# Three Strassen pairs for the attention projection of a decoder layer, with two of the four weight sums of each pair on GpSimd

## Chip, cores and metric

The kernel runs on one core of a Trainium2 chip. The metric is the device time of one execution in microseconds (us), the median of repeated runs. Times inside an execution are us from the start of its span.

## What is computed

One decoder layer over 256 tokens of width 1024, in float32. The part that matters here is the first half: a projection of the normalised tokens, two token mixers fed by it, and the joining of their outputs.

```python
xn = rms_norm(h, norm_mix[i])
proj = jnp.einsum('bsd,de->bse', xn, w_in[i])
gdn_qkv, gdn_z, gdn_a, gdn_b, fox_qkv, fox_f, merge = split_cols(proj, IN_SPLITS)
qkv = jax.nn.silu(causal_depthwise_conv(gdn_qkv, conv_w[i]))
...
o_a = gated_delta_rule(q_a, k_a, v_a, log_alpha, beta)
...
q_f = rms_norm(fox_qkv[..., :FOX_W].reshape(B, S, FOX_HEADS, FOX_HD), q_norm[i])
...
o_f = forgetting_attention(q_f, k_f, v_f, log_f)
...
h = h + jnp.einsum('bsd,de->bse', gate_a * y_a + gate_f * y_f, w_out[i])
h = h + routed_moe(...)
```

`fox_qkv` is the projection of the attention: 3072 columns, six weight tiles of 512 columns. `gated_delta_rule` needs, for each of 16 problems (8 heads, two chunks of 128 tokens), the inverse of a unit lower triangular matrix. The mixture of experts and a gated embedding follow, and fill the rest of the time.

## The kernel before

Each engine has its program written out by hand, in order; semaphores join them. Nothing is scheduled automatically: the order of the code in each engine's block is the order of execution, and a wait at the head of an engine's queue holds everything behind it.

**Weights.** Twenty-two tiles of 1024 rows by 512 columns (2 MB each) of the projections pass through a ring of three slots (`wring`, `A_SLOTS = 3`), filled by SyncE in `load(t)` (L466). A slot is filled again when its last reader on TensorE is done. Tiles 0 to 5 are the delta rule's q, k, v; tiles 6 to 11 the attention's; 12 and 13 the gate z; then the merge gates and the three output projections.

**Plain tiles.** In `project` (L1018) a weight tile is used twice, once for each 128 tokens: 8 chunks of the contraction, each one a 128x128 by 128x512 product. One such float32 product shows in the trace as two MATMUL records, so one `project` is 16 records. Before the change the attention's six tiles run this way: twelve `project` calls, fox.0.0 to fox.5.1, whose results ScalarE copies out of the accumulating bank.

**Paired tiles.** z, the merge gates and the output projections take two tiles at a time in a Strassen-Winograd form (`product`, L1028): seven half products of 4 chunks (8 records) instead of eight. They are named by number: 1, 5, 2, 6, 3, 7, 4 is their usual order. On VectorE `token_sums` makes four sums of token blocks once for each left factor, `weight_sum(p, k)` (L1848 to L1859) makes four sums of weight halves (128x2048 each) for every pair, and `join(p, k)` (L1869 to L1882) puts products together. ScalarE keeps products 1 and 5 in memory (`keep`). Product 5 waits for weight sum 1, product 6 for sum 2, product 7 for sum 3 and for join 6, product 4 for sum 4. Half products open banks A, C, B, D of a pair; a bank has to be drained before it is opened again.

**Beside the attention's tiles.** Between its products TensorE does small work for the delta rule (`BESIDE_FOX`: transposes tq, key products kk, spread rows bb, query products qk), which VectorE scales. Then, on VectorE, a **solve** of 31 steps inverts the sixty-four diagonal 32x32 blocks (L1825 and L1827, two small instructions a step, each waiting for the one before). SyncE brings the blocks through memory first (`box_blocks`, L490 and L492) and the inverses back (`unbox_inverses`, L497 and L502) into `xi` and `vi`, which GpSimd has set to zero (L667, L668). TensorE then completes the inverses by blocks (P5, X5, V5, P6, V6: L1187 and L1194), between z's seven products.

Of the kernel before, what the change touches and what calls it, by code (L numbers as in the profile page):

```python
# [41 lines left out]
def bc(ap, axis, n):  # L42
# [12 lines left out]
BESIDE_FOX = {(0, 0): ["tq.0.5", "tq.1.5", "kk.0", "kk.1"], (0, 1): ["bbT", "kk.2", "kk.3"],  # L55
              (1, 0): ["bb.0", "bb.1", "bb.2", "bb.3"], (1, 1): ["qk.0", "qk.1"], (2, 0): ["qk.2", "qk.3"]}

PAIRED = ("z", "m0", "m2", "ya", "yf", "wo")
Z_, M0_, M2_, YA_, YF_, WO_ = range(6)
LEFT = (0, 0, 0, 1, 2, 3)  # L60
# [11 lines left out]
def bank_fills():  # L72
# [8 lines left out]
    for j in range(6):  # L81
        for n in range(NT):
            f += [f"fox.{j}.{n}"] + BESIDE_FOX.get((j, n), [])
    f += ["cT", "P5", "z.A", "X5", "V5", "z.C", "P6.0", "P6.1", "V6.0", "V6.1", "z.B", "z.D"]
# [9 lines left out]
    g = [(name, ALL_BANKS) for name in f]  # L94
# [34 lines left out]
def program(nc, x, p, norm_mix, w_in, conv_w, a_log, dt_bias, gdn_norm, fox_f_bias, q_norm, k_norm,  # L129
# [3 lines left out]
    with ctx:  # L133
# [221 lines left out]
        ya_gated = sem("ya_gated")  # L355
        u_made, c11_made, activated = sem("u_made"), sem("c11_made"), sem("activated")
# [17 lines left out]
        wtiles += [(w_in2, C_FOX + WT * j, f"fox.{j}.1") for j in range(6)]  # L374
# [5 lines left out]
        W_QKV, W_FOX, W_PAIRED = 0, 6, 12  # L380

        def halves_of(p):

            k = W_PAIRED + 2 * p
            b0, b1 = wring[k % A_SLOTS], wring[(k + 1) % A_SLOTS]
            return b0[:, LO, :], b1[:, LO, :], b0[:, HI, :], b1[:, HI, :]

# [58 lines left out]
        def _(sp):  # L446
# [3 lines left out]
            def load(t):  # L450
# [43 lines left out]
            def unbox_inverses():  # L494
# [3 lines left out]
                sp.wait_ge(zeroed, 2)  # L498
# [70 lines left out]
            sp.wait_ge(t_made, 4 * WO_ + 4)  # L569
# [53 lines left out]
        def _(pool):  # L623
# [43 lines left out]
            g.memset(xi[:, :, :], 0.0).then_inc(zeroed, 1)  # L667
            g.memset(vi[:, :, :], 0.0).then_inc(zeroed, 1)  # L668
# [3 lines left out]

# [1701 lines left out]
```

## Time and profile before

| | |
|---|---|
| median of three runs | 905.59 us (905.34 to 906.22) |
| the profiled execution | 906.76 us, its span 905.0 us |
| TensorE busy | 893.1 us, 99% of the span |
| VectorE busy | 498.6 us, 55% |
| ScalarE busy | 198.1 us, 22% |
| GpSimd busy | 48.1 us, 5% |
| TensorE clock granted | 0.999 of full speed |

TensorE is never idle for long; its busy share says where the time is, but not whether another engine is nearly late. The stage of this change lies from about 104 to 229 us: the attention's projection up to 196 us, then z and the blocks of the inverses.

### The profile page before, as it was taken

How to read it: one execution, taken by the hardware profiler on the slowest of the kernel's cores; microseconds unless marked ns; L12 is line 12 of the kernel's file. 1: busy time of each engine (PE TensorE's matmuls, PEld its weight loads, DVE VectorE, ACT ScalarE, POOL GpSimd, SP SyncE). 2: the span in 40 equal slices, each digit the busy share in tenths (PEclk: the TensorE clock that was granted, in tenths of full speed). 3: DMA queues.
4: the chain of work that ended last, by engine and by line, in shares of the span. 5: the costliest groups of instructions: out<-in, count | busy, mean ns of one | idle time of the engine just before them, and what ended most of it. 6: DMA issues, size and time to landing. Idle time of an engine off the chain costs nothing.

```text
span 905.0 us, 21061 instructions
## 1 busy us (share of the span) xinstructions
PE 893.1 (99%) x9194; PEld 510.3 (56%) x9194; DVE 498.6 (55%) x954; ACT 198.1 (22%) x401; POOL 48.1 (5%) x72
## 2 busy tenths in 40 slices
PE   8999999999999999999999999999999999999997
PEld 6888755455845554446555555545455555555543
DVE  3656735964586887866434354443434444445367
ACT  2214200022417561233111111111111111111122
POOL 4011100050020000020000000000000000000010
PEclk9999999999999999999999999999999999999999
DMA  8643424562241528988999999999999999999951
GB/s 251 209 166 102 178 94 145 180 208 95 94 138 50 185 94 321 365 347 297 405 419 423 420 422 423 421 423 423 420 422 423 423 422 422 421 421 423 416 202 48
DMA packets 65587, 266.10 MB, mean 294 GB/s; under 512 B 11353, under 2 KB 14026, under 8 KB 41098
## 3 DMA queue, kind: packets, MB, share of 16 engines
q1 hardware_dynamic: 65530, 265.54, 74.4%
q8 instruction: 27, 0.44, 0.2%
q14 instruction: 14, 0.11, 0.0%
q10 hardware_dynamic: 16, 0.00, 0.0%
HBM read 263.69 MB, written 1.84 MB: 293 GB/s over the span
## 4 chain that ended last, share of the span: by engine, by line
PE 95%; DVE 2%; ACT 1%; issue 1%; DMA 0%; POOL 0%; DVEq 0%; ACTq 0%; POOLq 0%
PE bank L1493 25%; PE bank L1028 15%; PE bank L1474 13%; PE bank L1137 9%; PE bank L1018 9%; PE bank L1444 5%; PE bank L1457 5%; PE bank L1602 2%; PE bank L1005 2%; PE bank L1091 2%; PE bank L1513 1%; PE bank L1402 1%; PE bank L1413 1%; PE bank L1232 1%; PE bank L1330 1%; ACT arena L722 1%
## 5 line engine op out<-in xcount | busy, mean ns | idle before, releaser
L1493 PE MATMUL bank<-arena 128*32 128x256 f32 x4096 | 227.2, 379 | 0.3 <-DVE arena L2180 0.3
L1493 PEld LDWEIGHTS bank<-arena 128*32 128x32 f32 x4096 | 132.8, 110 | 100.5 <-issue 18.6
L1474 PE MATMUL bank<-arena 128*32 128x512 f32 x1024 | 116.5, 595 | 0.5 <-ACT arena L935 0.5
L1028 PE MATMUL bank<-arena 128*128 128x512 f32 x248 | 111.1, 598 | 0.0
L1137 PE MATMUL bank<-actT,arena 128*128 128x256 f32 x384 | 85.3, 380 | 0.0
L1018 PE MATMUL bank<-arena,actT 128*128 128x512 f32 x192 | 83.5, 593 | 0.0
L1137 PEld LDWEIGHTS bank<-actT,arena 128*128 128x128 f32 x384 | 72.0, 190 | 10.2 <-issue 0.8
L1028 PEld LDWEIGHTS bank<-arena 128*128 128x128 f32 x248 | 45.8, 190 | 53.9 <-issue 53.8
L933 ACT ACTIVATE arena<-bank 128x256 f32<-128x256 f32 x32 | 12.3, 384 | 267.9 <-PE bank L1493 267.9
L722 ACT ACTIVATE arena<-bank 128x512 f32<-128x512 f32 (+2 forms) x69 | 35.5, 534 | 154.5 <-PE bank L1018 82.7
L2231 DVE COPY arena<-bank 128x512 f32<-128x512 f32 x32 | 22.1, 692 | 81.9 <-PE bank L1474 81.9
L2216 DVE SCALAR_TENSOR_TENSOR arena<-arena,gslot,bank 128x256 f32<-128x256 f32 x32 | 15.4, 480 | 90.0 <-ACT arena L933 90.0
L1474 PEld LDWEIGHTS bank<-arena 128*32 128x32 f32 x1024 | 30.0, 109 | 59.9 <-issue 57.5
L1018 PEld LDWEIGHTS bank<-arena,actT 128*128 128x128 f32 x192 | 36.0, 190 | 43.2 <-issue 43.0
L2221 DVE COPY arena<-bank 128x512 f32<-128x512 f32 x31 | 21.4, 692 | 67.9 <-PE bank L1444 67.9
L1444 PE MATMUL bank<-onehot,arena 128*128 128x64 bf16 x1536 | 50.0, 193 | 0.0
L1444 PEld LDWEIGHTS bank<-onehot,arena 128*128 128x128 bf16 x1536 | 49.0, 98 | 1.0 <-issue 0.7
L2247 DVE TENSOR_TENSOR arena<-arena,masks 128x1024 f32<-128x1024 f32 x31 | 38.0, 1226 | 1.1
L653 POOL TENSOR_SCALAR stat<-stat 128x1 f32<-128x1 f32 x6 | 1.6, 268 | 617.7 <-ACT arena L971 468.3
L1005 PE MATMUL bank<-ident,arena 128*128 128x128 f32 (+1 forms) x206 | 29.4, 286 | 4.7 <-DMA arena<-in_norm_mix 3.3
L939 ACT ACTIVATE arena<-bank 128x512 f32<-128x512 f32 x32 | 19.1, 597 | 66.1 <-PE bank L1474 66.1
L1005 PEld LDWEIGHTS bank<-ident,arena 128*128 128x128 f32 (+1 forms) x206 | 25.1, 147 | 14.5 <-issue 10.6
(321 smaller groups left out, 1006.4 us busy)
## 6 DMA issues: line engine op xcount, KB each, us to landing
arena<-in_we_gate SPq DMA_DIRECT2D x32, 2048.0 KB, 17.3
arena<-in_we_up SPq DMA_DIRECT2D x31, 2048.0 KB, 18.5
arena<-in_we_down SPq DMA_DIRECT2D x29, 2048.0 KB, 17.5
arena<-in_w_in SPq DMA_DIRECT2D x17, 2048.0 KB, 8.1
arena<-in_we_down SPq DMA_DIRECT2D x6, 1024.0 KB, 8.9
arena<-in_w_branch_gdn SPq DMA_DIRECT2D x2, 2048.0 KB, 7.8
arena<-in_w_branch_fox SPq DMA_DIRECT2D x2, 2048.0 KB, 8.9
arena<-in_w_out SPq DMA_DIRECT2D x2, 2048.0 KB, 10.0
```

The costliest lines, as they stand in the source:

```text
L722: a.activation(dst, ps(name)[:, 0:cols_used] if len(dst.shape) == 2 else ps(name)[:, 0:cols_used].rearrange("p (a b) -> p a b", a=dst.shap ...
L1005: ins = t.transpose(o[0:w, i * P:i * P + rows_in], v, ident[0:rows_in, 0:rows_in])
L1018: ins = t.matmul(o[:, :], lhs[:, c, n * P:n * P + P], w[:, c, :], start=(c == 0), stop=(c == KC - 1))
L1028: ins = t.matmul(o[:, :], lhs[:, c, :], rhs[:, c, :], start=fresh and c == 0, stop=c == HC - 1, skip_group_check=not fresh)
L1137: ins = t.matmul(o[:, i * S:i * S + S], w[:, c, col:col + P], actT[:, c, :], start=(c == 0), stop=(c == KC - 1))
L1444: ins = t.matmul(bank[5 + half][:, c * P + n * 2 * CAP:c * P + (n + 1) * 2 * CAP], hparts[:, k, n, (4 * half + c) * P:(4 * half + c + 1) * P],
L1457: ins = t.matmul(bank[2 * n + j][:, :], spread[s][hp, :], yparts[j][k][hp, :], start=False, stop=False, skip_group_check=True)
L1474: ins = t.matmul(bank[4 + j][i * CAP:i * CAP + CAP, :], hidT[:, c, i * CAP:i * CAP + CAP], d_in[s][:, i % 2, c * D + WT * j:c * D + WT * j ...
L1493: ins = t.matmul(bank[4][i * CAP:i * CAP + CAP, m * DE:m * DE + DE], xg[:, c, i * CAP:i * CAP + CAP], gu_in[s][:, m, i % 2, c * DE:c * DE ...
L2221: v.tensor_copy(xg[:, 4:8, :], bank[6][:, :].rearrange("p (c s) -> p c s", c=4)).then_inc(xb_ready, 1)
L2231: v.tensor_copy(y[:, WT:D], bank[5][:, :]).then_inc(y_ready[1], 1)
L2247: v.tensor_tensor(y, y, yhigh, ALU.subtract).then_inc(y_rest, 1)
```

## The change

The attention's six tiles become three pairs f0, f2 and f4 with `product`, so that `project` is no longer used for them. The signs of the Strassen form are turned so that weight sums are all additions. For the three new pairs GpSimd makes weight sums 1 and 3 (`add_first`, `add_third`), VectorE makes sums 2 and 4. Banks are dealt out apart during the stage: 0, 1, 2 for the pairs and 3 to 7 for the work beside. On VectorE the solve is moved ahead of the scaling of the queries and keys (L1810 to L1817), and has joins and sums of the pairs between its steps. The zeroing of `xi` and `vi` is moved from the start to behind the pairs' last products, since the weight differences of f0 and f4 use the memory of `xi` and kept products of f2 that of `vi`. On TensorE product 1 of z now stands ahead of P5.

```diff
+FOX_BANKS, SIDE_BANKS = (0, 1, 2), (3, 4, 5, 6, 7)
+FOX_ORDER = ((0, 1, ["tq.0.5", "tq.1.5", "kk.0", "kk.1"]), (0, 2, []), (0, 5, ["bbT", "kk.2", "kk.3"]), (0, 6, []), (0, 3, ["bb.0", "bb.1", "bb.2", "bb.3"]),
+             (0, 7, ["qk.0", "qk.1"]), (0, 4, []), (1, 1, ["qk.2", "qk.3"]), (1, 5, []), (1, 2, []), (1, 6, []), (1, 3, []), (1, 7, []), (1, 4, []),
+             (2, 1, []), (2, 5, []), (2, 2, []), (2, 6, []), (2, 3, []), (2, 7, []), (2, 4, []))
...
+        wdif = [at(lo, HC * WT).rearrange("p (c n) -> p c n", c=HC) for lo in (TX, RZ, TX, R1, R1, TV, TPB, R1 + 2048)]
...
-            g.memset(xi[:, :, :], 0.0).then_inc(zeroed, 1)
-            g.memset(vi[:, :, :], 0.0).then_inc(zeroed, 1)
...
+            def add_first(p):
+                b00, b01, _, _ = halves_of(p)
+                for tile in (W_PAIRED + 2 * p, W_PAIRED + 2 * p + 1):
+                    pool.wait_ge(w_loaded[tile % A_SLOTS], 16 * (tile // A_SLOTS + 1))
+                g.tensor_tensor(wdif[p], b00, b01, ALU.add).then_inc(sum1_made, 1)
+
+            def add_third(p):
+                _, b01, _, b11 = halves_of(p)
+                pool.wait_ge(sum1_made, p + 1)
+                g.tensor_tensor(b01, b11, b01, ALU.add).then_inc(sum3_made, 1)
+
             for i, (j, n) in enumerate(TQ_ORDER):
+                if i == 6:
+                    add_first(F0_)
+                if i == 7:
+                    add_third(F0_)
...
+            add_first(F2_)
+            add_third(F2_)
+            wait_filled(pool, "f0.D")
+            add_first(F4_)
+            add_third(F4_)
+            pool.wait_ge(c11_made, F2_ + 1)
+            g.memset(vi[:, :, :], 0.0).then_inc(zeroed, 1)
+            wait_filled(pool, "f4.D")
+            g.memset(xi[:, :, :], 0.0).then_inc(zeroed, 1)
...
-            for j in range(6):
-                w = weights(W_FOX + j)
-                for n in range(NT):
-                    project(f"fox.{j}.{n}", w, n)
-                    for name in BESIDE_FOX.get((j, n), []):
-                        beside(name)
+            for p, k, names in FOX_ORDER:
+                product(p, k)
+                for name in names:
+                    beside(name)
...
+            product(Z_, 1)
             pe.wait_ge(xv_loaded, 16 * 2 * NB)
             corner32("P5", lambda b, q: (lT[q:q + BLK, b, q + BLK:q + 2 * BLK], q + BLK), lambda b, q: xi[q:q + BLK, b, q:q + BLK])
-            product(Z_, 1)
...
+            JOINED, SUMMED = {8: 6, 13: 3, 17: 7, 21: 4}, {24: 2, 27: 4}
+            for k in range(BLK - 1):
+                m = BLK - 1 - k
+                outer = rank1[:, 0:m * (k + 1)].rearrange("p (i j) -> p i j", i=m)
+                seq(v.tensor_tensor(outer, bc(lb[:, k, k + 1:BLK], 2, k + 1), bc(xb[:, k, 0:k + 1], 1, m), ALU.mult))
+                below = xb[:, k + 1:BLK, 0:k + 1]
+                seq(v.tensor_tensor(below, below, outer, ALU.subtract))
+                if k in JOINED:
+                    join(F2_, JOINED[k])
+                if k in SUMMED:
+                    weight_sum(F4_, SUMMED[k])
```

TensorE at the end of the attention's tiles, before (L1018 the last plain tile, L1011 the transpose cT, L1187 P5 and X5, L1028 z's product 1):

```order
L1018 MATMUL bank6<-arena,actT 128x512 [waits drained6]
L1018 MATMUL bank6<-arena,actT 128x512 x7
L1011 MATMUL bank7<-identb,cf3 48x128 [waits drained7,cf_split]
L1011 MATMUL bank7<-identb,cf3 48x128
L1187 MATMUL bank0<-arena 32x32 [waits drained0,xv_loaded]
L1187 MATMUL bank0<-arena 32x32 x31
L1028 MATMUL bank1<-arena,actT 128x512 [waits drained1,w_loaded0]
L1028 MATMUL bank1<-arena,actT 128x512 x3
L1187 MATMUL bank2<-arena 32x32 [waits drained2,drained0]
L1187 MATMUL bank2<-arena 32x32 x31
```

and the same place in the change (L1066 products, the first of them f4's product 4, L1049 cT, L1229 P5 and X5):

```order
L1066 MATMUL bank2<-arena,actT 128x512 [waits drained2,t_made]
L1066 MATMUL bank2<-arena,actT 128x512 x3
L1049 MATMUL bank4<-identb,cf3 48x128 [waits drained4,cf_split]
L1049 MATMUL bank4<-identb,cf3 48x128
L1066 MATMUL bank5<-arena,actT 128x512 [waits drained5,w_loaded0]
L1066 MATMUL bank5<-arena,actT 128x512 x3
L1229 MATMUL bank6<-arena 32x32 [waits drained6,xv_loaded]
L1229 MATMUL bank6<-arena 32x32 x31
L1229 MATMUL bank7<-arena 32x32 [waits drained7,drained6]
L1229 MATMUL bank7<-arena 32x32 x31
```

z's product 1 stood between P5 and X5; now it stands ahead of P5, and X5 (which waits for bank 6, P5's) follows P5 at once.

VectorE around the eighteenth step of the solve, before:

```order
L1825 TENSOR_TENSOR arena<-arena 64x252 [waits dve_step]
L1827 TENSOR_TENSOR arena<-arena 64x14x18 [waits dve_step]
L1825 TENSOR_TENSOR arena<-arena 64x247 [waits dve_step]
L1827 TENSOR_TENSOR arena<-arena 64x13x19 [waits dve_step]
L1825 TENSOR_TENSOR arena<-arena 64x240 [waits dve_step]
```

and in the change (L1928 and L1930 the steps, L1881 and L1884 join 7 of f2):

```order
L1928 TENSOR_TENSOR arena<-arena 64x252 [waits dve_step]
L1930 TENSOR_TENSOR arena<-arena 64x14x18 [waits dve_step]
L1881 TENSOR_TENSOR arena<-arena,bank0 128x512 [waits filled0,dve_step]
L1884 TENSOR_TENSOR arena<-arena 128x512 [waits drained0,kept]
L1928 TENSOR_TENSOR arena<-arena 64x247
L1930 TENSOR_TENSOR arena<-arena 64x13x19 [waits dve_step]
L1928 TENSOR_TENSOR arena<-arena 64x240 [waits dve_step]
```

Join 7 of f2, which drains bank 0 (f2.B, and next f4.C), now stands behind eighteen steps of the solve.

TensorE where the attention's tiles begin, before and (second fence) in the change; L1005 and L1043 are the transposes tq.1.4:

```order
L1005 MATMUL bank3<-ident,arena 128x128 [waits drained3,conv_done]
L1005 MATMUL bank3<-ident,arena 128x128 x3
L1018 MATMUL bank4<-arena,actT 128x512 [waits drained4,w_loaded0]
L1018 MATMUL bank4<-arena,actT 128x512 x7
L1005 MATMUL bank5<-ident,arena 128x128 [waits drained5,conv_done]
```

```order
L1043 MATMUL bank3<-ident,arena 128x128 [waits drained3,conv_done]
L1043 MATMUL bank3<-ident,arena 128x128 x3
L1066 MATMUL bank0<-arena,actT 128x512 [waits drained0,w_loaded0]
L1066 MATMUL bank0<-arena,actT 128x512 x3
L1043 MATMUL bank3<-ident,arena 128x128 [waits drained3,conv_done]
```

The first product of the stage opened bank 4; now it opens bank 0, whose last user is qkv.11, the last convolution tile.

## Rows read from the trace of the kernel before

**Rows 1.** The page's busy times of the engines.

```profile
PE 893.1 (99%) x9194; PEld 510.3 (56%) x9194; DVE 498.6 (55%) x954; ACT 198.1 (22%) x401; POOL 48.1 (5%) x72
```

**Rows 2.** The chain that ended last, in order of time: start, length, what.

```profile
104.21 6.87 PE bank L1018 x16
...
137.69 1.78 PE bank L1091 x16
...
148.13 48.07 PE bank L1018 x112
196.42 1.13 PE bank L1187 x64
197.55 3.63 PE bank L1028 x8
...
214.89 13.93 PE bank L1028 x32
```

**Rows 3.** VectorE's timeline ahead of the stage, and a weight load of SyncE.

```profile
98.86 2.48 DVE L1767 TENSOR_TENSOR arena<-arena,masks 128x512 f32<-128x512 f32 x4
...
103.74 2.54 DVE L1704 SCALAR_TENSOR_TENSOR arena<-bank,cols,arena 128x255 f32<-128x255 f32 x6
...
L466 SPq DMA_DIRECT2D arena<-in_w_in x1: 367/367/367, 88.2 to 88.2; - x1
```

**Rows 4.** VectorE's timeline: the solve, its copy, a weight sum, a join.

```profile
152.04 0.17 DVE L1825 TENSOR_TENSOR arena<-arena 64x31 f32<-64x31 f32 x1
...
165.28 0.41 DVE L1827 TENSOR_TENSOR arena<-arena 64x252 f32<-64x252 f32 x1
...
171.09 0.33 DVE L1827 TENSOR_TENSOR arena<-arena 64x175 f32<-64x175 f32 x1
...
174.67 0.18 DVE L1827 TENSOR_TENSOR arena<-arena 64x31 f32<-64x31 f32 x1
174.89 1.05 DVE L1828 COPY arena<-arena 64x1024 f32<-64x1024 f32 x1
...
192.22 2.29 DVE L1848 TENSOR_TENSOR arena<-arena 128x2048 f32<-128x2048 f32 x1 [3.82 <-DMA arena<-in_w_in]
...
218.63 0.69 DVE L1869 TENSOR_TENSOR arena<-arena,bank 128x512 f32<-128x512 f32 x1 [3.44 <-PE bank L1028]
```

**Rows 5.** GpSimd's timeline, and the VectorE instruction beside its last row.

```profile
11.25 1.80 POOL L667 MEMSET arena<- 128x2048 f32 x1
...
190.62 5.44 POOL L685 TENSOR_TENSOR f_ri<-f_ri,nhalf 128x32 f32<-128x32 f32 x1
247.31 0.22 POOL L689 TENSOR_TENSOR stat<-stat 128x16 f32<-128x16 f32 x1 [51.26 <-DVE stat L1939]
247.61 2.29 POOL L690 TENSOR_TENSOR stat<-stat 128x16 f32<-128x16 f32 x1
...
247.53 2.29 DVE L1855 TENSOR_TENSOR arena<-arena 128x2048 f32<-128x2048 f32 x1 [0.30 <-PE bank L1028]
```

**Rows 6.** SyncE's timeline, landings of transfers, and a page row of loads.

```profile
138.27 5.22 SPq L490 DMA_DIRECT2D lbox<-arena  x4
147.06 0.54 SPq L492 DMA_DIRECT2D arena<-lbox  x1
...
180.12 1.93 SPq L502 DMA_DIRECT2D arena<-xbox  x4
182.09 2.08 SPq L502 DMA_DIRECT2D arena<-vbox  x4
...
DMA to landing us min/median/max: 2.0/2.3/2.5
...
arena<-in_w_in SPq DMA_DIRECT2D x17, 2048.0 KB, 8.1
```

**Rows 7.** ScalarE's timeline: the two copies that drain P5.

```profile
197.60 1.19 ACT L774 ACTIVATE arena<-bank 32x512 f32<-32x512 f32 x2 [0.77 <-PE bank L1187]
```

More of the change, by code:

```diff
@@ L373, in program @@
         wtiles = [(w_in2, C_QKV + WT * t, f"qkv.{2 * t + 1}") for t in range(6)]
-        wtiles += [(w_in2, C_FOX + WT * j, f"fox.{j}.1") for j in range(6)]
+        wtiles += [(w_in2, C_FOX + WT * j, f"f{j // 2 * 2}") for j in range(6)]
         wtiles += [(w_in2, C_Z + WT * j, "z") for j in range(2)]
@@ new lines, in weight_sum @@
+            def weight_sum(p, k):
+                b00, b01, b10, b11 = halves_of(p)
+                if k == 1:
+                    for i in range(2):
+                        tile = W_PAIRED + 2 * p + i
+                        dve.wait_ge(w_loaded[tile % A_SLOTS], 16 * (tile // A_SLOTS + 1))
+                    ins = v.tensor_tensor(wdif[p], b01, b00, ALU.add)
+                if k == 3:
+                    dve.wait_ge(t_made, sums_made(p, 1))
+                    ins = v.tensor_tensor(b01, b11, b01, ALU.add)
+                if k == 2:
+                    if p < Z_:
+                        tile = W_PAIRED + 2 * p + 1
+                        dve.wait_ge(w_loaded[tile % A_SLOTS], 16 * (tile // A_SLOTS + 1))
+                        dve.wait_ge(sum1_made, p + 1)
+                    else:
+                        dve.wait_ge(t_made, sums_made(p, 1))
+                    dve.wait_ge(half_filled, 3 * p + 1)
+                    ins = v.tensor_tensor(b00, b11, wdif[p], ALU.add)
+                if k == 4:
+                    dve.wait_ge(t_made, sums_made(p, 2))
+                    dve.wait_ge(half_filled, 3 * p + 2)
+                    ins = v.tensor_tensor(wdif[p], b10, b00, ALU.add)
+                ins.then_inc(t_made, 1)
@@ L1884, in _, with fox_squares @@
-            token_sums(LEFT[Z_])
+            join(F4_, 3)
+            join(F4_, 7)
+            join(F4_, 4)
+            for p in (F0_, F2_):
+                for q in "ACBD":
+                    wait_drained(dve, f"{PAIRED[p]}.{q}")
+            dve.wait_ge(c11_made, F2_ + 1)
+            def fox_squares(n, half):
+                src = fox[:, n, D * half:D * half + D]
+                seq(v.tensor_tensor(at(TPB, 1024), src, src, ALU.mult))
+                ins = v.tensor_reduce(f_ss[:, n, 16 * half:16 * half + 16], at(TPB, 1024).rearrange("p (a b) -> p a b", a=16), AX.X, ALU.add)
+                if half:
+                    ins.then_inc(fss, 1)
+                    dve.wait_ge(fss, n + 1)
+                else:
+                    seq(ins)
@@ L1885, in _ @@
+            weight_sum(Z_, 1)
+            weight_sum(Z_, 3)
             for n in range(NT):
                 for half in range(2):
-                    for j in range(2):
-                        wait_drained(dve, f"fox.{2 * half + j}.{n}")
-                    src = fox[:, n, D * half:D * half + D]
-                    seq(v.tensor_tensor(at(TPB, 1024), src, src, ALU.mult))
-                    ins = v.tensor_reduce(f_ss[:, n, 16 * half:16 * half + 16], at(TPB, 1024).rearrange("p (a b) -> p a b", a=16), AX.X, ALU.add)
@@ L1893, in _ @@
[L1893 to L1899 removed]
+                    fox_squares(n, half)
             wait_filled(dve, "cT")
@@ L2090, in _ @@
             dve.wait_ge(kept, 2 * WO_ + 1)
-            k = [step(onto(n, j, m1[WO_])) for n, j in BLOCKS[1:]]
+            k = [step(onto(n, j, m1[WO_], ALU.subtract if j else ALU.add)) for n, j in BLOCKS[1:]]
             wait_filled(dve, "wo.A")
```

194 lines of the change are left out of this document (95 added, 99 removed).

## The prediction

> **What bounds the kernel now.** I read the page's busy times first: TensorE works for 99% of the span [rows 1]. So only two things count, how much work TensorE loses, and how long it newly waits. The chain of work in order of time gives both scales for this stage [rows 2]. A plain tile half (16 records) takes 6.87 us; the stage begins at 104.21 and its last seven come in one piece of 48.07 us, 6.87 each. The half products of z take 3.48 us each when they follow one another (13.93 for four) and 3.63 between small work. Then I read the timelines of the others, for what could be late.
>
> **The work removed.** Twelve plain halves, 12 x 6.87 = 82.4 us, become 21 half products, 21 x 3.48 = 73.1. TensorE gains 9.3 us. Nothing else in the stage leaves TensorE; the work beside (91.99 from 104.21 to 196.20, less 82.4: 9.6, of which the last piece takes 1.8) is the same.
>
> **The work added elsewhere.** VectorE gets four token sums (only moved), six weight sums of 2.29 us and fifteen instructions of 0.69 for joins [rows 4], about 24 us more. ScalarE makes six copies more and eight fewer. What follows asks where TensorE waits. Times are on the clock of the trace of before.
>
> 1. *Entry.* f0.A opens bank 0, which qkv.11 used last. VectorE drains that with six instructions that end at 103.74 + 2.54 = 106.28 [rows 3]; TensorE arrives at 104.0. Before, bank 4 was long free. Wait: **2.3 us**.
>
> 2. *Exit, zeroing.* `xi` can only be zeroed once product 4 of f4 is complete, and SyncE's eight transfers into `xi` and `vi` wait for it. 0.2 release, 1.80 for the memset [rows 5], 0.1, then issues: eight, from 180.12 to 184.17, the last landing about 2.3 after its issue, 5.9 in all [rows 6]. Sum 8.0. TensorE has cT (0.22) and z's product 1 (3.63) as cover, 3.85. Wait: **4.2 us**. Before, both memsets were done at 15 us and the inverses were back 10 us ahead of P5 (186 against 196.42).
>
> 3. *Exit, P5.* X5 waits for ScalarE's two copies of P5, 1.19 us [rows 7], plus 0.26 for two releases. z's product 1 covered them and now stands ahead. Wait: **1.45 us**.
>
> 4. *Solve and joins.* The solve starts behind f2's product 5 and sum 4. With the entry's wait, TensorE starts f2's product 5 at 106.3 + 24.4 (seven products) + 7.7 (work beside) + 3.5 (f2's product 1) + 1.8 (the last piece beside) = 143.8; it ends at 147.3, the sum at 149.7. SyncE's boxes are no obstacle: started at about 133, they are in at the latest 13.8 us later (138.27 to 152.04). The eighteen steps before join 7 take 165.69 - 152.04 = 13.65 [rows 4], the joins at steps 8 and 13 0.7 each, join 7 itself 0.7: bank 0 is free at about 165.5. TensorE wants it for f4's product 5 at 143.8 + 7 x 3.48 = 168.1. Margin 2.6 us (2.3 with releases): no wait, but nothing to spare. At the end f4's join 6 stands behind the last steps, sum 4 and the copy, about 7.5 us after sum 2, where TensorE has two products, 6.96. Wait: **0.5 us**.
>
> 5. *Two GpSimd adds per pair.* No such instruction is in the trace. Lower bound of one: the memset of the same shape, 1.80, which moves one operand where an add moves three [rows 5]; upper bound three passes, 5.4. Reads alone through one door would make two, 3.6. I take 4.5, midway between two and three passes. By time alone they fit: f4's second tile is requested after f2's product 6 (154.2), lands 8.1 later [rows 6], sum 1 is ready at 166.8, wanted at 168.1.
>
> What matters is whether they leave VectorE alone. At 247.61 a GpSimd multiply of 128x16, whose neighbour took 0.22, took 2.29: it ended with VectorE's two-input sum that had started at 247.53 [rows 5]. So the two share something that one holds to its end. Whether GpSimd holds it against VectorE too is the open point. For it: the sharing is complete in the case seen. Against: VectorE's sum at 192.22 took its normal 2.29 while a GpSimd power ran from 190.62 to 196.06 [rows 4, 5]. But that one reads 32 elements and then computes; an add of 2048 reads nearly all the time. I take it that the long add does hold. The Trainium skill, "SBUF — State Buffer", section "Who interferes with whom", speaks against this change: a VectorE instruction with two SBUF inputs and a GpSimd one that reads SBUF exclude each other for the whole instruction, whoever starts first. The trace agrees in one direction (2.29 for 0.22), and shows no long GpSimd read for the other. For the length, "GPSIMD Engine Reference", section 3.1, gives 4.497 us for this very add (by it the sum would be the same), and no run here shows it yet.
>
> The price of holding:
> - f0's first add starts when its tile lands, about 96, and holds until 100.5. VectorE's four two-input instructions at 98.86 [rows 3] start 1.6 late; 0.9 of it is idle time before the last convolution. Entry wait **+0.7**.
> - f2's adds fall among scaling instructions with one SBUF input; they shift one join's last part and sum 2, and cost the solve's start 0.4 at most.
> - f4's adds (162.3 to 171.4) fall into the solve, where nearly every instruction has two SBUF inputs. VectorE stands still for 2 x 4.5 = 9.0. Join 7 is 9.0 later, less the margin of 2.3: f4's product 5 waits **6.7**. From join 7 to the end of sum 2 VectorE needs 0.7 + 5.7 (steps 18 to 24, to 171.42) + 0.7 + 2.29 = 9.4, against two products, 6.96: product 6 waits **2.5**.
>
> **Sum.** Without holding: -9.3 + 2.3 + 4.2 + 1.45 + 0.5 = -0.9. With it: -0.9 + 0.7 + 6.7 + 2.5 = +9.0. The profiled execution of before took 906.76, 1.2 over the median of 905.59; its like after would be 915.8, and the median **914.6 us**.
>
> **Rivals.**
> - *GpSimd's add holds nothing* (chance 0.25). For it: the power of 190.62. Against: the complete wait at 247.61. The kernel is then not slower: 905.6 - 0.9 = **904.7**, and TensorE's waits are those of 1 to 4. It decides from a hold of about 1.2 us per add on; below that the margin of 2.3 swallows it.
> - *More is late than that* (0.12): an add of 5.4 (+0.9 on each of two, and f2's product 7 then waits 0.7 too) and tiles landing 1 us later since the boxes' transfers run beside them: +12.5, **918.1**. For it: the loads now come in twos. Against: 8.1 was measured with pauses between and beside boxes too.
> - *The gain shows after all* (0.06): if waits 2 and 3 were covered, by transfers landing as a group rather than one by one, 905.6 - 0.9 - 3 = **901.7**. Against: the eight issues themselves take 4.05 us.
> - That the seven-for-eight exchange does not happen has no chance worth a number: the counts of products are in the program.
>
> **Numbers.** The forecast has 0.57. Its own range is 911 to 917 (adds of 3.6 to 5.0). The whole range reaches to the case without holding and leaves out the edges: 904 to 918.5. A change of this kernel can be told from none at about 0.2%, 1.8 us. Slower by more: 0.57 + 0.12 = 0.69; within: nearly all of the 0.25, 0.23; faster: 0.06 and a tail of the second, 0.08.
>
> **What the profile after would show.** Right: TensorE idle 3 us at its first half product of the stage, released by VectorE's convolution; GpSimd adds of 4.5 us (start to start); during the two of f4 VectorE's small solve instructions stretched to 4.5 us each, twice; TensorE waiting about 7 us at f4's product 5 for VectorE's join 7; 4 us ahead of P5 for a transfer; 1.5 ahead of X5 for ScalarE. If the solve's instructions keep their 0.4 us beside GpSimd's adds, the first rival holds. If P5 starts within 4 us of cT, step 2 is wrong. If the first product waits for nothing, step 1 is. If the half products take 3.63 rather than 3.48, the gain is 3 us smaller.

## The result, and the profile after

| | before | after |
|---|---|---|
| median of four runs | 905.47 us (905.22 to 906.22) | 919.31 us (919.05 to 919.68) |
| ratio | 1 | 1.0152, 95% interval 1.0140 to 1.0164 |
| profiled execution, its span | 906.76, 905.0 us | 919.38, 917.7 us |
| TensorE clock granted, mean | 0.999 | 0.987 |
| TensorE busy | 893.1 us, 99% | 891.7 us, 97% |

The change makes the kernel 1.5% slower. The forecast was 914.6 us, and its range ended at 918.5: the sign was right, the size too small by 4.7 us. Of the runs further below, one of the four executions of e10_tuned took 1856.62 us and is in none of its figures.

The page of the changed kernel, its busy times and the clock in 40 slices of 22.9 us. [Rows 1] have the first line before.

```profile
PE 891.7 (97%) x9170; PEld 510.3 (56%) x9170; DVE 534.3 (58%) x975; ACT 196.3 (21%) x398; POOL 76.2 (8%) x78
...
PEclk9999999897999999999999999999999999999999
```

TensorE has 1.4 us less to do by its busy time although seven half products stand for eight, since some of its work ran longer: in two slices, from 161 to 184 and from 206 to 229 us, the clock digit is not 9.

TensorE's waits in the whole program, summed by line and releaser. The rows left out are before the stage (2.3 and 1.6 us) and after it, and one of 0.9 ahead of the last record of V5 (214.30), which the account below has in the length of X5 and V5.

```profile
PE bank L1066 <- DVE arena L1881: 5.8, 1, 5.8
PE bank L1229 <- DMA arena<-vbox: 4.1, 1, 4.1
PE bank L1066 <- DVE arena L1746: 2.8, 1, 2.8
...
PE bank L1229 <- ACT arena L801: 1.3, 1, 1.3
```

They are the waits of the prediction, in its places: join 7 of f2, the transfers into `vi`, the last convolution (L1746), ScalarE's copies of P5. Its TensorE timeline in the stage (L1043 transposes, L1066 half products, L1229 P5, X5 and V5); [rows 2] have the same places before:

```profile
103.55 1.47 PE L1043 MATMUL bank<-ident,arena 128*128 128x128 f32 x12
107.77 3.67 PE L1066 MATMUL bank<-arena,actT 128*128 128x512 f32 x8 [2.75 <-DVE arena L1746]
...
174.92 6.72 PE L1066 MATMUL bank<-arena 128*128 128x512 f32 x8 [5.83 <-DVE arena L1881]
181.47 3.60 PE L1066 MATMUL bank<-arena,actT 128*128 128x512 f32 x8
184.91 10.46 PE L1066 MATMUL bank<-arena 128*128 128x512 f32 x24
...
206.76 1.92 PE L1229 MATMUL bank<-arena 32*32 32x32 f32 x64 [4.10 <-DMA arena<-vbox]
209.96 3.44 PE L1229 MATMUL bank<-arena 32*32 32x32 f32 x127 [1.29 <-ACT arena L801]
...
214.43 5.75 PE L1066 MATMUL bank<-arena 128*128 128x512 f32 x8
220.12 2.08 PE L1236 MATMUL bank<-arena 64*64 64x64 f32 x32
...
241.59 0.60 PE L1043 MATMUL bank<-ident,arena 128*128 128x128 f32 x4
```

Read the starts, not the lengths: f4's product 5 starts at 174.92 and the next at 181.47, 6.55 us, where three others take 10.30 together (184.91 to 195.21). z's product 5 takes 5.69 (214.43 to 220.12). X5 and V5 take 4.47 (209.96 to 214.43). The clock of those stretches (columns: stretch, length, busy time and records of PE, PEld, DVE, ACT, POOL, the clock, DMA share, GB/s):

```profile
174.90:181.50 6.60, 6.58 (x9) 2.75 (x10) 6.15 (x16) 0.00 (x0) 1.81 (x1) 0.53 0.01 2
181.50:203.00 21.50, 21.16 (x51) 8.95 (x49) 18.07 (x27) 1.50 (x3) 1.81 (x1) 1.00 0.39 129
203.00:206.70 3.70, 0.00 (x0) 0.00 (x0) 3.63 (x4) 0.29 (x1) 0.00 (x0) 0.76 0.84 122
206.70:214.40 7.70, 5.46 (x192) 5.09 (x192) 7.50 (x8) 2.36 (x4) 5.27 (x2) 0.50 0.70 264
214.40:220.10 5.70, 5.70 (x9) 2.23 (x8) 2.10 (x1) 1.18 (x2) 5.53 (x3) 0.63 0.01 3
```

Before each of the two long waits ends the granted clock falls to 0.5, the level of 1.2 GHz (in windows of 1 us: at about 174.2 and 204.9). It is back at 1.00, 2.4 GHz, only at about 181, 6 us into product 5, and at about 218.6, 12 us behind the second wait. This the prediction had not priced. The VectorE and GpSimd timelines of the same execution show who made TensorE wait; [rows 4] have the solve before, [rows 3] the instruction at 98.86 before (2.48):

```profile
99.66 4.13 DVE L1809 TENSOR_TENSOR arena<-arena,masks 128x512 f32<-128x512 f32 x4
...
163.00 0.42 DVE L1928 TENSOR_TENSOR arena<-arena 64x256 f32<-64x256 f32 x1
163.45 4.62 DVE L1930 TENSOR_TENSOR arena<-arena 64x256 f32<-64x256 f32 x1
168.10 4.60 DVE L1928 TENSOR_TENSOR arena<-arena 64x255 f32<-64x255 f32 x1
...
174.09 0.69 DVE L1881 TENSOR_TENSOR arena<-arena,bank 128x512 f32<-128x512 f32 x1
```

```profile
163.27 4.52 POOL L684 TENSOR_TENSOR arena<-arena 128x2048 f32<-128x2048 f32 x1 [19.50 <-DMA arena<-in_w_in]
167.87 4.56 POOL L689 TENSOR_TENSOR arena<-arena 128x2048 f32<-128x2048 f32 x1
...
198.87 1.81 POOL L712 MEMSET arena<- 128x2048 f32 x1 [21.43 <-PE bank L1066]
```

A solve instruction that takes 0.42 us takes 4.62 and its successor 4.60: each ends 0.3 us behind the GpSimd add beside it (those end at 167.79 and 172.43). Join 7 follows at 174.09, and its first half ends where TensorE's wait does.

**The account.** For a measure that the rest of the program does not touch I take the stage, from the twelve transposes ahead of it to the transposes tg behind z. Before:

```profile
102.74 1.47 PE L1005 MATMUL bank<-ident,arena 128*128 128x128 f32 x12
...
201.11 1.83 PE L1187 MATMUL bank<-arena 32*32 32x32 f32 x109
...
203.55 3.70 PE L1028 MATMUL bank<-arena 128*128 128x512 f32 x8
...
228.66 0.60 PE L1005 MATMUL bank<-ident,arena 128*128 128x128 f32 x4
```

That is 228.66 - 102.74 = 125.92 us before and 241.59 - 103.55 = 138.04 after, +12.12. The stage itself began 0.81 later; TensorE's program ahead of it is the same in both.

| term, us | predicted | measured |
|---|---|---|
| entry wait | 2.3 + 0.7 | 2.75 |
| f4's product 5 waits | 6.7 | 5.83 |
| f4's product 5 at the slower clock | 0 | 6.55 - 3.44 = 3.11 |
| products 6 and 7 wait | 2.5 + 0.5 | 0 |
| wait ahead of P5 | 4.2 | 4.10 |
| wait ahead of X5 | 1.45 | 1.29 |
| P5 slower (1.91 for 1.13) | 0 | 0.78 |
| X5 and V5 slower (4.47 for 2.44) | 0 | 2.03 |
| z's product 5 slower (5.69 for 3.63) | 0 | 2.06 |
| sum of these | 18.35 | 21.95 |
| seven half products for eight | -9.3 | 12.12 - 21.95 = -9.8 |

A half product takes 3.44 us from start to start (10.30 / 3), so the exchange should give 82.4 - 21 x 3.44 = 10.2; 9.8 is what is left over. In each further profile below, the waits and slow products, less this 9.8, make the measured stage within 0.4 us.

### The profile page after: what moved, and what is told of

It reads as the page before. It is cut to its first block, busy times and chain, and to the rows that moved or that the text cites. A ratio compares the mean times of both kernels' runs of the same rounds, so it can differ in the third digit from the quotient of the medians.

```text
span 917.7 us, 21076 instructions
## 1 busy us (share of the span) xinstructions
PE 891.7 (97%) x9170; PEld 510.3 (56%) x9170; DVE 534.3 (58%) x975; ACT 196.3 (21%) x398; POOL 76.2 (8%) x78
## 4 chain that ended last, share of the span: by engine, by line
PE 90%; DVE 6%; ACT 1%; issue 1%; DMA 1%; POOL 0%; SPq 0%; DVEq 0%; ACTq 0%; POOLq 0%
PE bank L1535 24%; PE bank L1066 21%; PE bank L1516 12%; PE bank L1181 8%; PE bank L1486 5%; PE bank L1499 5%; PE bank L1644 2%; PE bank L1043 2%; PE bank L1135 2%; PE bank L1555 1%; DVE arena L1930 1%; DVE arena L1928 1%; PE bank L1444 1%; PE bank L1455 1%; PE bank L1274 1%
## 5 line engine op out<-in xcount | busy, mean ns | idle before, releaser
L1066 PE MATMUL bank<-arena 128*128 128x512 f32 x344 | 158.8, 613 | 5.8 <-DVE arena L1881 5.8
L1066 PEld LDWEIGHTS bank<-arena 128*128 128x128 f32 x344 | 65.6, 195 | 85.8 <-issue 85.5
L1066 PE MATMUL bank<-arena,actT 128*128 128x512 f32 x144 | 65.0, 596 | 2.8 <-DVE arena L1746 2.8
L753 ACT ACTIVATE arena<-bank 128x512 f32<-128x512 f32 (+2 forms) x60 | 30.1, 524 | 84.1 <-PE bank L1043 40.9
L1066 PEld LDWEIGHTS bank<-arena,actT 128*128 128x128 f32 x144 | 26.6, 190 | 33.8 <-issue 33.6
L1043 PE MATMUL bank<-ident,arena 128*128 128x128 f32 (+1 forms) x206 | 29.4, 286 | 4.3 <-DMA arena<-in_norm_mix 2.3
L807 ACT ACTIVATE arena<-bank 128x512 f32<-128x512 f32 x18 | 10.7, 595 | 106.2 <-PE bank L1066 106.2
L977 ACT ACTIVATE arena<-bank 128x512 f32<-128x512 f32 x32 | 19.1, 597 | 66.1 <-PE bank L1516 66.1
```

The lines of the kernel that those rows point to most:

```text
L753: a.activation(dst, ps(name)[:, 0:cols_used] if len(dst.shape) == 2 else ps(name)[:, 0:cols_used].rearrange("p (a b) -> p a b", a=dst.shap ...
L977: a.activation(y[:, 0:WT], bank[4][:, :], ACT.Copy).then_inc(y_ready[0], 1)
L1043: ins = t.transpose(o[0:w, i * P:i * P + rows_in], v, ident[0:rows_in, 0:rows_in])
L1066: ins = t.matmul(o[:, :], lhs[:, c, :], rhs[:, c, :], start=fresh and c == 0, stop=c == HC - 1, skip_group_check=not fresh)
```

## The experiments

All edits are to the changed kernel. "Stage" is the profiled length between the same two groups of transposes.

| run | median, us (lowest to highest) | ratio to before | stage, us |
|---|---|---|---|
| after | 919.31 (919.05 to 919.68) | 1.0152 | 138.04 |
| e1_short | 909.98 (908.88 to 910.96) | 1.0048 (1.0032 to 1.0065) | 129.88 |
| e2_long | 909.52 (909.16 to 909.93) | 1.0044 (1.0027 to 1.0061) | 130.39 |
| e11_copy | 911.44 (910.46 to 914.13) | 1.0059 (1.0037 to 1.0082) | 132.64 |
| e4_xi | 917.29 (916.06 to 920.0) | 1.0126 (1.0110 to 1.0143) | 139.43 |
| e5_fill | 916.74 (914.84 to 917.92) | 1.0129 (1.0112 to 1.0146) | 135.32 |
| e3_bank | 917.58 (916.06 to 918.34) | 1.0125 (1.0101 to 1.0148) | 136.67 |
| e6_vadds | 916.36 (914.04 to 917.1) | 1.0108 (1.0082 to 1.0134) | 136.87 |
| e8_order | 911.35 (909.12 to 911.96) | 1.0061 (1.0040 to 1.0082) | 129.86 |
| e9_all | 902.09 (901.71 to 903.55) | 0.9963 (0.9948 to 0.9977) | 122.37 |
| e10_tuned | 901.82 (900.32 to 902.49) | 0.9941 (0.9922 to 0.9961) | 122.88 |

The kernel before ran beside each group: 905.18, 905.23 and, beside e10 and e11, 906.38 us.

### Does GpSimd's add hold VectorE, and what in it does?

**e1_short**: the adds become one memset each.

```diff
-                g.tensor_tensor(wdif[p], b00, b01, ALU.add).then_inc(sum1_made, 1)
+                g.memset(wdif[p], 0.0).then_inc(sum1_made, 1)
...
-                g.tensor_tensor(b01, b11, b01, ALU.add).then_inc(sum3_made, 1)
+                g.memset(b01, 0.0).then_inc(sum3_made, 1)
```

> Each of the six GpSimd adds is replaced by one GpSimd memset of the same 128x2048 target, which reads nothing; all waits and signals stay. The kernel leaves out the three pairs' first and third weight sums. Theory A, that the long add holds VectorE: VectorE's solve instructions keep 0.42 us, join 7 of f2 is 9 us earlier, f4's product 5 waits for nothing and takes 3.44 to 3.5 us, the entry wait falls from 2.75 to 2.1, while the waits ahead of P5 (4.1) and X5 (1.3) and the slow stretch behind them stay. That takes off 5.8 + 3.1 + 0.7 = 9.6: 919.3 - 9.6 = 909.7 us, 908.5 to 911. Rival B, that f2's joins are late for another reason (the solve begins late, the loads are late, or TensorE is slow there of itself): 917 us or more, with the same 5 us wait.

**e2_long**: three memsets, longer than the add but without a read.

```diff
-                g.tensor_tensor(wdif[p], b00, b01, ALU.add).then_inc(sum1_made, 1)
+                for i in range(3):
+                    ins = g.memset(wdif[p], 0.0)
+                    if i < 2:
+                        seq(ins)
+                ins.then_inc(sum1_made, 1)
...
```

> Each of the six GpSimd adds is replaced by three memsets of its target one after the other (3 x 1.8 = 5.4 us, longer than the add's 4.5), still without any read. The kernel leaves out the three pairs' first and third weight sums. Theory A, that it is the two reading inputs of the GpSimd instruction that hold VectorE's: no VectorE instruction is stretched, f4's weight sums come 1.8 us later, which costs f4's product 5 at most 1 us: 909.7 to 911.5 us. Rival B, that any GpSimd instruction that occupies its engine so long holds VectorE, or that the length of the sums is what is waited for: 5.4 instead of 4.5 us held twice, 919.3 + 2 = 921 us or more.

**e11_copy**: one input instead of two.

```diff
-                g.tensor_tensor(wdif[p], b00, b01, ALU.add).then_inc(sum1_made, 1)
+                g.tensor_copy(wdif[p], b00).then_inc(sum1_made, 1)
...
-                g.tensor_tensor(b01, b11, b01, ALU.add).then_inc(sum3_made, 1)
+                g.tensor_copy(b01, b11).then_inc(sum3_made, 1)
```

> The changed kernel with each of the six GpSimd adds replaced by a GpSimd copy of the same size (one input instead of two). The kernel leaves out the three pairs' first and third weight sums, and copies one operand instead. It tells what in GpSimd's reading holds VectorE. Theory A, any GpSimd instruction that reads holds VectorE's two-input instructions to its end: solve instructions stretched to the copy's own length (1.8 to 3.6 us by the memset's 1.8 and the add's 4.5), f4's product 5 waits the less the shorter the copy is; at 3 us twice: 919.3 - 2 x 1.5 = 916 us, 914 to 917.5. Theory B, only two reading inputs hold: no instruction is stretched, as with memsets: 909 to 911 us.

Measured: 909.98, 909.52 and 911.44. With memsets both theory A held, 0.3 us from its value in e1 and 0.2 below its range in e2, and both rivals fell. GpSimd's timeline in e2, three memsets that begin at 162.56 (three more follow at 168.15), and a VectorE row beside them, one of twenty-odd alike:

```profile
162.56 5.53 POOL L685 MEMSET arena<- 128x2048 f32 x3 [16.09 <-DMA arena<-in_w_in]
```

```profile
162.36 0.42 DVE L1936 TENSOR_TENSOR arena<-arena 64x256 f32<-64x256 f32 x1
```

Eleven microseconds of GpSimd work stretch nothing; in e1 and e2 f4's product 5 has no wait. In e11 GpSimd's copy for f4's sum 1 (the one for sum 3 follows at 164.65 with 1.97), then VectorE's two instructions beside the two copies:

```profile
162.69 1.90 POOL L684 COPY arena<-arena 128x2048 f32<-128x2048 f32 x1 [23.51 <-DMA arena<-in_w_in]
```

```profile
162.77 2.08 DVE L1930 TENSOR_TENSOR arena<-arena 64x256 f32<-64x256 f32 x1
164.89 1.99 DVE L1928 TENSOR_TENSOR arena<-arena 64x255 f32<-64x255 f32 x1
```

One input is enough: VectorE's two-input instruction is held for the copy's whole 1.9 us. So theory A of e11 is right in its mechanism and B is wrong; its time was off because the copy is hardly longer than a memset (1.90 for 1.80 us), and 911.44 lies outside both ranges, 0.4 above B's: the time alone would not have told the two apart, the stretched instructions do. With 2.08 + 1.99 us instead of 4.62 + 4.60, f4's product 5 waits 0.7 for join 7, and product 6 shows the wait for sum 2, 2.2 us. The Trainium skill, "SBUF — State Buffer", section "Who interferes with whom", states just this condition, that a two-input VectorE instruction contends only with a GpSimd one that reads SBUF. These runs agree in all three cases: 0.42 us beside memsets, 2.08 beside a copy, 4.62 beside an add. One row does not fit the condition, and decides there: the GpSimd power reads SBUF too, and from 190.62 to 196.06 it held nothing, since VectorE's sum at 192.22 took its usual 2.29 [rows 4, 5]. Which GpSimd instructions hold to their end is shown here only for the add and the copy of 128x2048.

### Are the slow products the clock?

**e5_fill**: work that nothing reads stands in the two long waits.

```diff
             for p, k, names in FOX_ORDER:
+                if (p, k) == (F4_, 5):
+                    wait_drained(pe, "bb.3")
+                    for _ in range(56):
+                        t.transpose(bank[3][:, 0:P], ident[:, :], ident[:, :])
                 product(p, k)
...
             product(Z_, 1)
+            wait_drained(pe, "bb.3")
+            for _ in range(36):
+                t.transpose(bank[3][:, 0:P], ident[:, :], ident[:, :])
             pe.wait_ge(xv_loaded, 16 * 2 * NB)
```

> TensorE gets work that nothing uses in the two long waits: 56 transposes of 128x128 ahead of f4's product 5, 36 ahead of P5, into a bank that is free, with the waits themselves unchanged. Nothing is left out. Theory, that the slow products behind the waits (f4's product 5 at 6.55 instead of 3.44 us, X5 and V5 at 4.5 instead of 2.4, z's product 5 at 5.7 instead of 3.6) are the granted clock of an engine that has stood still: they come back to full speed in part or whole, and the granted clock stays at 0.9 or over there. Of the 8.0 us so lost, the 3.1 at f4's product 5 cover waits for sum 2 and join 6 of 2.5 + 0.5, so they give only 0.1 to 0.6; the other 4.9 are free. 919.3 - 5.3 = 914 us; 913 to 916. Rival, that the products are slow from something else (contention with transfers or with VectorE's work): no change, 919.3 us or more.

Measured 916.74 (the profiled execution 914.84), mean clock 0.996 for 0.987. Its TensorE timeline:

```profile
167.10 6.28 PE L1220 MATMUL bank<-ident 128*128 128x128 f32 x56
173.21 3.60 PE L1066 MATMUL bank<-arena 128*128 128x512 f32 x8
176.65 3.60 PE L1066 MATMUL bank<-arena,actT 128*128 128x512 f32 x8
182.38 12.23 PE L1066 MATMUL bank<-arena 128*128 128x512 f32 x24 [2.14 <-issue]
...
208.25 2.32 PE L1233 MATMUL bank<-arena 32*32 32x32 f32 x128 [1.29 <-ACT arena L801]
210.50 5.11 PE L1066 MATMUL bank<-arena 128*128 128x512 f32 x8
```

Where TensorE was kept at work until the wait ended, what follows is at full speed: product 5 takes 3.44 again, P5 1.20, X5 and V5 2.25. That the slow products are the clock, and the clock follows from the standing still, is shown; contention is out, since the work of VectorE, GpSimd and the transfers beside them is the same. Two more things are to be seen. Product 6 now waits 2.14 us for sum 2: this is the prediction's 2.5, which in the changed kernel was hidden behind the slow product 5. And the clock falls behind the shorter waits instead: 1.76 at product 6 (12.07 to the next start, for 10.31), 1.4 at z's product 5. So the filling gave back less than the 5.3 us expected: 2.6 by the medians, 0.7 above the theory's range, and 2.7 of the stage.

The Trainium skill, "TensorE: Matmul & The Clock Gate", section "HAM oscillation — how this bites in real kernels", describes that each burst behind a wait for data starts at the lower level. The windows above agree for the two long waits: 0.53 and 0.50 behind 5.8 and 4.1 us, where the page's two levels would be 0.5 and 1. They don't for every wait: the first half product behind 2.75 us ran at 1.00.

### The exit

**e4_xi**: `xi` is zeroed early.

```diff
-        wdif = [at(lo, HC * WT).rearrange("p (c n) -> p c n", c=HC) for lo in (TX, RZ, TX, R1, R1, TV, TPB, R1 + 2048)]
+        wdif = [at(lo, HC * WT).rearrange("p (c n) -> p c n", c=HC) for lo in (TX, RZ, R1, R1, R1, TV, TPB, R1 + 2048)]
...
             wait_filled(pool, "f0.D")
+            g.memset(xi[:, :, :], 0.0).then_inc(zeroed, 1)
+            wait_filled(pool, "qk.3")
             add_first(F4_)
...
-            wait_filled(pool, "f4.D")
-            g.memset(xi[:, :, :], 0.0).then_inc(zeroed, 1)
```

(Its sum tile went to R1, which z's own sum tile uses later, not to f2's RZ as the expectation has it, and f4's sum 1 waits for qk.3 as well. What the place itself does to the time was not tried; e9 has RZ.)

> The sum tile of f4 moves from xi's place to the one f2 used, so that xi can be zeroed by GpSimd once product 4 of f0 is done (ahead of f4's sums) instead of product 4 of f4; the adds stay. Theory: the wait ahead of P5 (4.1 us) is gone since the transfers of xi and vi land some 6 us earlier, and the half-speed clock behind it goes with it (0.8 in P5, 2.0 in X5 and V5, 2.1 in z's product 5). The 1.3 us wait for ScalarE stays, with some of the clock loss perhaps. 919.3 - 4.1 - 4.9 = 910.3 us; 909.5 to 912.5. Rival, that the fall of the clock at 203 comes late from the 5.8 us wait at 169 to 175 and not from the waits at 203 to 210: only the wait goes, 915.2 us.

Measured 917.29: two microseconds of nine, and neither the theory's range nor the rival's 915.2. The wait ahead of P5 fell only from 4.10 to 2.02, and what follows was as slow as before (X5 and V5 4.75 us, z's product 5 6.69). (The profiled execution is the slowest of the four, 920.0: its first half product was slow, 5.20 us, and f4's product 5 waited 6.43.) SyncE's timeline of e4 (L506 fetches the finished inverses, L511 puts them into `xi` and `vi`):

```profile
190.07 0.37 SPq L475 DMA_DIRECT2D arena<-in_w_in  x1
...
192.73 0.60 SPq L506 DMA_DIRECT2D vbox<-arena  x1
199.94 1.93 SPq L511 DMA_DIRECT2D arena<-xbox  x4
```

and the time to landing of the transfer into `vbox` (a row of the DMA view), in e4 and then before:

```profile
vbox<-arena SPq DMA_DIRECT2D x1, 256.0 KB, 7.2
```

```profile
vbox<-arena SPq DMA_DIRECT2D x1, 256.0 KB, 3.6
```

Behind the zeroing stood a second thing that was late: the inverses leave VectorE 9 us late, and now run behind a weight tile of 2 MB issued 2 us earlier, so they need 7.2 us where they needed 3.6. Before, the last tile had been issued 7.2 us ahead of them and was just in (the DMA traffic of it ends at 176.0, the inverses are issued at 175.97 and 176.48). That the tile is the cause rests on eleven profiles of this order against that one: where it is issued 2.2 to 2.4 us ahead of the first of the two transfers, they take 6.1 to 7.2 us; in e5 and e6, where it is 1.1, they take 7.4 to 8.4. No run moves the tile alone. In the changed kernel they landed at 198.1, 2.5 us ahead of the zeroing's end, and nothing of this showed.

**e8_order**: another order on TensorE, and VectorE's sums for z moved up with it.

```diff
-            product(Z_, 1)
+            for k in (1, 5, 2):
+                product(Z_, k)
             pe.wait_ge(xv_loaded, 16 * 2 * NB)
...
+            product(Z_, 6)
             wait_drained(pe, "P5")
...
-            product(Z_, 5)
             wait_drained(pe, "X5")
...
-            product(Z_, 2)
+            product(Z_, 3)
             wait_drained(pe, "V5")
...
-            for k in (6, 3, 7, 4):
+            for k in (7, 4):
                 product(Z_, k)
```

> The exit is written in another order, nothing is left out and f0, f2 and f4 stay as they are: z's products 1, 5 and 2 stand ahead of P5 (three half products of cover, 10.4 us, where there was one), z's product 6 between P5 and X5, product 3 between P6 and V6; VectorE makes z's sums 1, 3 and 2 ahead of the sums of squares. Theory: the waits ahead of P5 (4.1 us) and X5 (1.3) are covered and the granted clock stays at full speed there (4.9 us): 919.3 - 10.3 = 909.0 us, 908 to 911. Rival, that waits of this size only move (z's product 5 or 6 waits for its weight sum, or product 7 for join 6): 912 to 916 us.

Measured 911.35, -8.0, 0.35 above the theory's range. Its timeline has no wait at P5 (209.47), and one of 0.37 behind X5 and V5 (214.23):

```profile
209.47 1.20 PE L1229 MATMUL bank<-arena 32*32 32x32 f32 x64
...
214.23 2.12 PE L1229 MATMUL bank<-arena 32*32 32x32 f32 x128
216.72 2.08 PE L1236 MATMUL bank<-arena 64*64 64x64 f32 x32 [0.37 <-ACT arena L801]
```

Of the 10.3 us expected, 9.9 went from the exit (all but this 0.37). In this profile 1.7 came back at the entry, where the first half product behind the same wait (2.77 us) took 5.21 us, not 3.51; by the medians the gain is 8.0.

### The entry and the solve

**e3_bank**: `FOX_BANKS` is (1, 0, 2) instead of (0, 1, 2).

> Only the order of the first two banks of the attention's projection is exchanged, so that f0's first half product opens a bank that had been free for long, not the one that qkv.11 leaves late. Theory: the 2.75 us wait ahead of the first half product is gone and nothing takes its place, since all that is late further on is set by TensorE's own products: 919.3 - 2.75 = 916.6 us, 915.9 to 917.3. Rival, that the wait also served as slack (the adds and the loads of f2 and f4 are then late against TensorE by so much more): between 918 and 919.3 us, with a longer wait at f4's product 5.

Measured 917.58, -1.7 of the 2.75, and 0.3 above the theory's range. The wait of 2.75 is gone from the profile; 0.39 for a copy of ScalarE (L753) and 0.46 for VectorE's scaling of the values (L1818), which the longer wait had covered, came in its place. f4's product 5 waits as long as before (5.82), so the rival has no part in it.

**e6_vadds**: f4's sums 1 and 3 on VectorE.

```diff
-            add_first(F4_)
-            add_third(F4_)
...
+                if k == 17:
...
+                    v.tensor_tensor(wdif[F4_], b00, b01, ALU.add).then_inc(sum1_made, 1)
+                if k == 22:
...
+                    v.tensor_tensor(b01, b11, b01, ALU.add).then_inc(sum3_made, 1)
```

> f4's first and third weight sums go from GpSimd to VectorE, between two steps of the solve (2.29 us each); f0's and f2's stay on GpSimd. Nothing is left out. Theory, holding: VectorE gains 9.0 us of stretched time and pays 4.6 for the sums; no solve instruction is at 4.6 us, f4's product 5 does not wait and is at full clock (-5.8 - 3.1), a wait of about 1.0 for sum 2 and one of 0.8 for join 6 appear: 919.3 - 8.9 + 1.8 = 912.2 us, 910.5 to 914. Rival, that VectorE's plain amount of work is what is late, so that moving 4.6 us onto it costs: 918 us or more.

Measured 916.36, -3.0 where -7 was expected. The hold is gone, but sum 2 stands behind both new sums ("issue" is written where the profile shows no releaser; by the program, product 5 waits for sum 1 and product 6 for sum 2):

```profile
170.03 3.67 PE L1064 MATMUL bank<-arena 128*128 128x512 f32 x8 [1.02 <-issue]
...
180.78 12.23 PE L1064 MATMUL bank<-arena 128*128 128x512 f32 x24 [3.64 <-issue]
```

Waits of 1.02 and 3.64 and 1.76 us of slower clock take the place of 5.83 + 3.11, and the entry's first product ran at the lower clock (another 1.7). Neither theory had it right: the hold cost, and so does VectorE's plain work once it stands ahead of sum 2.

### All together

**e9_all**: e3 and e8, `xi` zeroed early with f4's sum tile in RZ, and f4's sums 1 and 3 on VectorE, at steps 18 and 25 of the solve, the third behind sum 2.

> All remedies at once, nothing left out: the banks exchanged, xi zeroed early (f4's sum tile in f2's place), f4's sums 1 and 3 on VectorE in the solve, and the exit in the new order. If the account of the loss is complete (entry 2.75, f4's product 5 8.9, exit 10.3), 919.3 - 21.9 = 897.4 us, plus up to 2 for VectorE's added 4.6 us: 896.5 to 900, which is the gain of seven products for eight (9.3 us) below the kernel before. Rival, that the gain of the exchange is itself smaller than 9.3 us, or that VectorE becomes the limit of this stage: 901 to 905 us.

Measured 902.09, ratio 0.9963: faster than the kernel before by 3.1 us, and 2.1 us over the upper end expected, in the range of the rival that VectorE becomes the limit. TensorE's waits from 100 to 240 us, the two largest (three of 0.4 follow):

```profile
PE bank L1063 <- issue: 1.9, 1, 1.9
PE bank L1063 <- DVE arena L1872: 1.4, 1, 1.4
...
```

4.5 us of waits and 1.8 of slower clock behind the first of them (f4's product 5): -9.8 + 6.3 = -3.5, and the stage is 122.37 - 125.92 = -3.55. So the exchange's gain is there in full, and of the 6.3 us lost 5.1 stand at f4's products 5 and 7, which wait for VectorE's sum 1 and join 6.

**e10_tuned**: f2's join 7 and f4's sum 1 at step 15, sum 2 at step 20, sum 3 at step 23, join 6 at step 26.

> The kernel with all remedies, with VectorE's order in the solve changed for the two waits that its profile still shows (1.9 us at f4's product 5 for sum 1, with 1.9 more by the slower clock behind it, and 1.4 at product 7 for join 6): f2's join 7 and f4's sum 1 two to three steps earlier, sum 2 at step 20, sum 3 at step 23, join 6 at step 26. Nothing is left out. Theory: 902.1 - 1.9 - 1.9 - 1.4 = 896.9, less what now falls on P5 (up to 1 us for the inverses, which do not come earlier): 897 to 899 us. Rival, that VectorE has no room left and the waits reappear at products 6 or 4 or at z's product 5: 900 to 902 us.

Measured 901.82, ratio 0.9941 against a run of before that was itself at 906.38: by the medians 0.3 us better than e9, by the profiled stages (122.88 and 122.37) no better. Its waits at f4's products 5 and 7 are gone (0.44 at product 6 is left), as expected, and two things took their place:

```profile
192.58 3.67 PE L1063 MATMUL bank<-arena 128*128 128x512 f32 x8 [1.78 <-issue]
...
206.87 2.75 PE L1233 MATMUL bank<-arena 64*64 64x64 f32 x32 [0.37 <-ACT arena L798]
209.55 6.31 PE L1063 MATMUL bank<-arena 128*128 128x512 f32 x8
```

z's product 5 waits for z's sum 1, whose weight tile lands at 190.2: TensorE arrives earlier, the tile does not. And P6 and z's product 3 ran at a mean clock of 0.71 and 0.58, 3.3 us lost, behind a wait of only 0.37. The rival had the time and the place right, but what is late there is the tile; VectorE stood idle for it for 1 us.

## Why the prediction was right in its steps and wrong in its sum

- **The work removed**: right. -9.3 predicted, -9.8 left over by the account; e9 and e10 confirm it within 0.2. The half product was priced at 3.48 us, a length that has the tail of the last one in it; from start to start it is 3.44.
- **Step 1, entry**: right, 2.75 for 2.3 + 0.7. L1809's four instructions took 4.13 for 2.48, 1.65 us late by the hold (1.6 predicted); without the hold the wait is 2.2 (e1, e2). e3 shows it worth 1.7, not 2.75, since 0.85 of other waits stood right behind.
- **Step 2, zeroing of `xi`**: right in size (4.10 for 4.2) and chain, but it was the latest of two things, not the only one; e4.
- **Step 3, ScalarE's copies**: right, 1.29 for 1.45.
- **Step 4, margin of the solve**: right. Without the hold (e1, e2) f4's product 5 waits for nothing.
- **Step 5, the adds**: right. 4.52 to 4.86 us for 4.5; they hold VectorE, 4.62 + 4.60; product 5 waits 5.83 for 6.7, since each held instruction loses the add's length less its own 0.4 us (4.20 and 4.19, together 8.4, where 2 x 4.5 = 9.0 was charged) and the margin was 2.6, not 2.3; the wait of 2.5 for sum 2 is 0 in the changed kernel and 2.1 once product 5 is at full clock (e5). "GPSIMD Engine Reference" of the Trainium skill, section 3.1, had 4.497 us for this add; the trace agrees with 4.52.
- **The sum: the step that failed.** Every product behind a wait was priced at its full-clock duration. The sum has no term for TensorE's granted clock, although it puts waits of 6.7 and 5.7 us into an engine that had stood at 0.999. Measured: 3.1 at f4's product 5, 4.9 from P5 to z's product 5, together 8.0. Against it stand 4.4 us by which the waits are smaller than predicted (14.0 for 18.35; 3.0 of it is what the slow product 5 covers) and 0.5 more of gain: 8.0 - 4.4 - 0.5 = 3.1, the stage's +12.1 for +9.0. That the miss is no larger is luck: what went the other way, none of it foreseen, took 4.9 of the 8.0 us. The rest of the 4.7 us is no step: the stage began 0.8 later, the program behind it took 0.3 less, and the profiled execution of before stood 1.2 above its median of then, that of after 0.1.
- **The range**: the rival "more is late" priced a longer add and later tiles; neither came. Its 918.1 came by another road than the one that led to 919.3. The rival that the add holds nothing fell with the stretched instructions and with e1, e2 and e11, the one with covered waits at the exit with the 4.10 and 1.29 us measured there.

What stays open is when exactly the clock falls. The same first half product behind 2.75 to 2.79 us of waiting ran at full speed in two profiles (3.51 us to the next start, after and e5) and slowed in three (5.2 in e6, e8 and e4); behind 2.2 us it ran at full speed in e1 and slowed in e2 and e11; and in e10 the clock fell behind 0.37. Why it falls in one and not in another was not settled here.

## What to carry to other kernels

A wait of some microseconds on an engine that had none costs more than its length: price the products behind it at the lower clock level too, here 1.7 to 3.1 us for a wait ahead of full products where the clock fell, and look in the windows for the clock, not only in the list of waits. Before weight sums or other elementwise work go to GpSimd, ask what VectorE does meanwhile: beside the memsets it lost nothing, and beside an add or a copy of 128x2048 its two-input instruction stood until the GpSimd one was done. And a wait that is removed uncovers the next late thing: ask what was ready only just ahead of it (here transfers issued just behind a weight tile), and reorder for cover (e8) rather than speed up one link (e4).

## What the hardware showed that I had not expected

- A GpSimd copy of 128x2048 took 1.90 us, hardly longer than a memset of that size (1.80); an add of two such inputs took 4.52. Two inputs cost more than twice one.
- A one-input GpSimd copy held VectorE's two-input instruction until it was done, 2.08 us for 0.42; three memsets in a row, 5.53 us, did not at all.
- Transfers of 256 KB issued 2.2 and 2.7 us behind a 2 MB tile landed after 6.4 and 7.2 us, against 2.9 and 3.6 where the tile had been issued 7.2 and 7.7 us ahead.
- Behind waits of 3.6 to 6.5 us the granted clock was at the lower level each time, at once or within 3 us; behind waits of 0.4 to 2.8 us only sometimes.
- The start of the stage lay between 101.5 and 103.6 us in twelve profiles whose TensorE program ahead of it is the same.
